# The prompt part of a hybrid GLA/MLA decoder step: stacked gate products, rope halves swapped by transfers, one fewer copy of the samples' queries

## The chip, the cores and the metric

One NeuronCore of a Trainium2 chip runs the kernel; the other cores are idle. The metric is device time in microseconds (us) of one execution, the median of several runs. TensorE does the matrix products, VectorE (DVE in the rows) and ScalarE (ACT) read its results out of the accumulator memory PSUM, GpSimd (POOL) and SyncE (SP) mostly issue transfers (DMA).

## What is computed

One decoder layer with two parallel head groups on one normed input `n` (512 prompt tokens, 16 meta tokens, 8 sample tokens of running sequences; width 1024), in single precision. Cut to what matters here:

```python
q, k, v, gr, g, cq, ckv, kpe = jnp.split(n @ w_in, idx, axis=-1)
lg = log_sigmoid((gr @ w_gk + b_gk)) / 16                  # gate logits, rank 16 -> 4 x 64
qh = (_rmsnorm(cq, q_norm) @ w_uq).reshape(B, T, 4, 128 + 64)
q_lat = einsum('bthn,rhn->bhtr', qh[..., :128], w_uk)
q_pe = _rope(qh[..., 128:])     # x1, x2 = halves: [x1*cos - x2*sin, x1*sin + x2*cos]
ckv, kpe = _rmsnorm(ckv, kv_norm), _rope(kpe)
# then chunked linear attention with the cumulative sums of lg, causal latent attention
# over the prompt, latent attention of the 8 samples over 4096 cached rows each (paged),
# merge by w_out, SwiGLU feed-forward, final norm
```

## The kernel before, in words

Everything stays in one fixed program per engine, ordered by hand; engines meet through semaphores. Big products are made exact enough by splitting both operands into a high and a low part of type fp32r and adding three products (high*high, low*high, high*low): `dense` (L753 to 763), `two_layers` (L766 to 778), `by_token` (L794 to 796) and `dense_piece` (L901 to 922). Each of those moves 256 to 268 columns and is one record in the trace. A plain fp32 product is two records. A weight block of 256 columns is loaded by SyncE (`load_block`), ScalarE copies its high part (`hi`, L1403) and VectorE subtracts for the low part (`lo`, L1776); two block buffers alternate, and `use(n)` on TensorE waits for `lo(n)`.

PSUM is used as four pairs of banks. `plan` writes down every result ("fill") in order and gives each the next pair in turn; `take(name)` on TensorE waits until the pair's earlier fill was read out (`free` on the reader), and `evacuated(name)` waits until a fill was read.

TensorE's order in the prompt part, which the change touches:

- transposes of the normed input (`xT`, L814), then `cq0` to `cq2` (the query latent);
- `tok0` to `tok2` (latent rows), then `ssq`: the sum over features of the squares of `cq`, made by multiplying three tiles of squares with a matrix of ones (`ones_sum`, L804, 6 products), then `tok3`, `tok4`;
- `kr` (rope part of the keys and the 16 gate features in one fill; ScalarE takes the key rows at L1451, VectorE the gate features into `grT` at L1830, which frees the pair), `wuk0`, `wuk1` and `kp` (transposes, L842 and L848);
- the gate logits `lg0` to `lg4`: one plain fp32 product per 128 tokens, 17 rows deep (16 features and a row of ones against the bias), 256 columns (L852). ScalarE and VectorE read each and go on to log-sigmoid;
- `qn0`, `qn1`, `qp0`, `qn2`, `qn3`, `qp1`: the queries of the heads, 18 split products each. ScalarE copies `qp` into `qpe` (L1466);
- small transposes (`cks`, `ck2`, L868 and L872), the samples' latent queries `qlat` (L880), then `sw0`, `sw1`: `qpe` multiplied by a permutation matrix so that the rope halves swap (L886, four plain fp32 products of 260 columns, 8 records); VectorE multiplies by sine and cosine and adds (L1860 to 1863) and signals `qpe_done`;
- the gates' cumulative sums `b0` to `b4` (L895);
- `q0` (48 split products as eight pieces), then `qx` (L940 and L945): the samples' queries spread over 128 rows, written twice, into two banks, 12 narrow fp32 products each, so that VectorE (L1882) and ScalarE (L1494) can each read its own bank and fill `Qall`; then `q1` (48 split products), then `snew` (L953);
- the loop over the cached rows, 16 steps (L968, L977, L991), with the products for `k`, `v` in between, fed by GpSimd's gathers of cache rows into a ring of six buffers (`gather_latent` L649, `gather_rope` L654).

What stands in the other queues around this: SyncE loads block 7, stores the latent rows (12 transfers, L528 and L529), and then waits for `q1` to load block 8. GpSimd fetches `w_gk` and `b_gk` (L659, L660), gathers the first rope rows once `ctok_done` is there, waits for `qpe_done`, clears two buffers (L665, L666) and then gathers on. VectorE runs in the order: gate logits, `lo(6)`, copies of `cks`, `ck2`, `qlat`, the rotation, `lo(7)`, transposes of cached keys (`cache_keys`, L1875), `Qall`.

## Time and profile before

| What | us |
|---|---|
| median of 3 runs | 862.75 |
| the three runs | 859.09, 863.98, 862.75 |
| the profiled execution, its own time | 864.38 |
| its span, first to last instruction | 862.6 |
| mean granted TensorE clock, as a share of full speed | 0.958 |

The profiled execution is one more run with the hardware profiler on; its span lies inside its own time. The page gives busy times by engine, the span in 40 slices, the chain of work that ended last and the costliest groups of instructions. Where the granted clock of a stretch is 1.00 TensorE runs at 2.4 GHz, where it is 0.50 at 1.2 GHz. A busy time of TensorE counts overlapping records once.

### The profile page before, as it was taken

To read this page: it belongs to the slowest core of one execution; us is meant where nothing else is said; L and a number is where in the kernel's file an instruction comes from. 1 tells how busy PE (TensorE), PEld (TensorE's weight loads), DVE (VectorE), ACT (ScalarE), POOL (GpSimd) and SP (SyncE) were. 2 spreads that over 40 slices of the span, in tenths; PEclk is the share of its full clock that TensorE was granted. 3 is DMA by queue.
4 is the path that set the end of the run, shared out by engine and by line. 5 is a ranking of instruction groups with operands and counts; after the bars stand their busy time and mean duration, and the time that the engine had idled before them with its cause. 6 is when DMAs were issued, how large, how long until landed. Compare 5 with 4: busy or idle time off the path is not lost.

```text
span 862.6 us, 20177 instructions
## 1 busy us (share of the span) xinstructions
PE 803.0 (93%) x8886; PEld 756.0 (88%) x8886; DVE 442.6 (51%) x596; ACT 268.8 (31%) x428; POOL 124.6 (14%) x147
## 2 busy tenths in 40 slices
PE   1999988788888899999999999999999999999997
PEld 1998987667776699788999999999999999999996
DVE  4344638676686556868346444445544454123223
ACT  5234312111123344545545322222222222223113
POOL 5101314343451022630000000000000000000000
PEclk9998979999999999689999999999999999999998
DMA  8525165876883022033431333322223332222202
GB/s 259 176 55 156 60 234 213 307 267 225 320 337 104 8 67 60 2 99 121 133 99 50 99 97 97 97 96 73 78 94 97 97 97 87 86 98 86 85 0 99
DMA packets 72160, 105.95 MB, mean 123 GB/s; under 512 B 7584, under 2 KB 63960, under 8 KB 67872
## 3 DMA queue, kind: packets, MB, share of 16 engines
q1 hardware_dynamic: 64528, 62.89, 23.2%
q0 software_dynamic: 7568, 42.11, 13.1%
q8 instruction: 52, 0.85, 0.4%
q14 instruction: 12, 0.10, 0.0%
HBM read 100.99 MB, written 4.00 MB: 122 GB/s over the span
## 4 chain that ended last, share of the span: by engine, by line
PE 85%; DVE 7%; issue 4%; ACT 2%; DMA 1%; SPq 0%; ACTq 0%; DVEq 0%
PE pair L776 10%; PE pair L777 10%; PE pair L778 10%; PE pair L761 8%; PE pair L762 8%; PE pair L763 8%; PE pair L968 4%; PE pair L991 2%; DVE KT L1875 2%; PE pair L1190 2%; PE pair L794 2%; PE pair L795 1%; PE pair L796 1%; PE pair L814 1%; DMA X<-in_x_prompt 1%
## 5 line engine op out<-in xcount | busy, mean ns | idle before, releaser
L776 PE MATMUL pair<-xhi,whi 128*128 128x260 f32 x736 | 209.2, 284 | 0.4 <-ACT rsf L1704 0.4
L777 PE MATMUL pair<-xlo,whi 128*128 128x260 f32 x736 | 208.6, 283 | 0.0
L778 PE MATMUL pair<-xhi,wlo 128*128 128x260 f32 x736 | 208.6, 283 | 0.0
L776 PEld LDWEIGHTS pair<-xhi,whi 128*128 128x128 f32 x736 | 139.6, 190 | 0.7 <-issue 0.6
L777 PEld LDWEIGHTS pair<-xlo,whi 128*128 128x128 f32 x736 | 139.6, 190 | 0.0
L778 PEld LDWEIGHTS pair<-xhi,wlo 128*128 128x128 f32 x736 | 139.5, 189 | 0.0
L763 PE MATMUL pair<-hhi,wlo 128*128 128x260 f32 x352 | 99.4, 282 | 0.0
L761 PE MATMUL pair<-hhi,whi 128*128 128x260 f32 x352 | 99.3, 282 | 0.0
L762 PE MATMUL pair<-hlo,whi 128*128 128x260 f32 x352 | 99.2, 282 | 0.0
L1875 DVE STREAM_TRANSPOSE KT<-KC 128x2048 uint32<-128x2048 uint32 x32 | 73.7, 2303 | 0.0
L2219 DVE TENSOR_TENSOR wlo<-wraw,whi 128x2048 fp32r<-128x2048 f32 x22 | 50.4, 2293 | 38.7 <-ACT whi L1724 38.7
L761 PEld LDWEIGHTS pair<-hhi,whi 128*128 128x128 f32 x352 | 66.3, 188 | 0.0
L762 PEld LDWEIGHTS pair<-hlo,whi 128*128 128x128 f32 x352 | 66.2, 188 | 0.0
L763 PEld LDWEIGHTS pair<-hhi,wlo 128*128 128x128 f32 x352 | 66.1, 188 | 0.0
L2244 DVE TENSOR_TENSOR wlo<-wraw,whi 128x2048 fp32r<-128x2048 f32 (+1 forms) x10 | 20.8, 2079 | 75.9 <-ACT whi L1736 75.9
L968 PEld LDWEIGHTS pair<-KT,Qall 128*32 128x32 f32 x2048 | 32.3, 110 | 21.9 <-DVE KTp L1876 10.0
L968 PE MATMUL pair<-KT,Qall 128*32 128x64 f32 x2048 | 37.8, 221 | 14.1 <-issue 7.8
L1719 ACT ACTIVATE hhi<-fe 128x520 f32 x22 | 13.7, 639 | 106.7 <-DVE fe L2232 106.7
L649 POOL DMA_INDIRECT KC<-in_cache_ckv,icur x32 | 31.3, 979 | 77.2 <-issue 72.1
L1724 ACT ACTIVATE whi<-wraw 128x2048 fp32r<-128x2048 f32 x22 | 41.8, 1902 | 0.0
L1776 DVE TENSOR_TENSOR wlo<-wraw,whi 128x2048 fp32r<-128x2048 f32 (+2 forms) x12 | 23.5, 1956 | 33.4 <-ACT whi L1403 33.3
L654 POOL DMA_INDIRECT KP<-in_cache_kpe,icur x32 | 31.4, 982 | 54.1 <-DVE ctok L1840 44.6
(351 smaller groups left out, 1671.0 us busy)
## 6 DMA issues: line engine op xcount, KB each, us to landing
wraw<-in_w_gate SPq DMA_DIRECT2D x11, 1024.0 KB, 5.3
wraw<-in_w_up SPq DMA_DIRECT2D x11, 1024.0 KB, 5.3
wraw<-in_w_down SPq DMA_DIRECT2D x8, 1024.0 KB, 5.2
X<-in_x_prompt SPq DMA_DIRECT2D x8, 512.0 KB, 5.6
wraw<-in_w_in SPq DMA_DIRECT2D x4, 1024.0 KB, 6.0
wsame<-in_w_in SPq DMA_DIRECT2D x4, 1024.0 KB, 6.2
wraw<-in_w_down SPq DMA_DIRECT2D x4, 768.0 KB, 4.8
wsame<-in_w_out SPq DMA_DIRECT2D x2, 1024.0 KB, 6.6
```

The source lines that it names most:

```text
L649: g.indirect_dma_start(KC[x][:, :], None, ckv_rows, bass.IndirectOffsetOnAxis(icur[x][:, 0:1], 0)).then_inc(S(f"kc_loaded{x}"), 16)
L654: g.indirect_dma_start(KP[x][:, :], None, kpe_rows, bass.IndirectOffsetOnAxis(icur[x][:, 0:1], 0)).then_inc(S(f"kc_loaded{x}"), 16)
L761: mm(out, wcols(h, j), hi[:, kx, tok], start=first and j == 0, stop=False)
L762: mm(out, wcols(h, j), lo[:, kx, tok], start=False, stop=False)
L763: ins = mm(out, wcols(l, j), hi[:, kx, tok], start=False, stop=last and j == len(k_of) - 1)
L776: mm(out, h[:, k, c], xhi[:, k, tok], start=k == order[0], stop=False)
L777: mm(out, h[:, k, c], xlo[:, k, tok], start=False, stop=False)
L778: ins = mm(out, l[:, k, c], xhi[:, k, tok], start=False, stop=k == order[-1])
L968: ins = mm(pairs[2][32 * t:32 * t + 32, o:o + 64], Qall[:, n // 2, 32 * c:32 * c + 32], kk, start=c == 0, stop=c == NBLK - 1)
L1724: f(whi[n % 2][:, :], wraw[n % 2][:, :], ACT.Copy).then_inc(w_hi, 1)
L1875: v_.transpose(KT[y][:, :, :, :].rearrange("p u c j -> p (u c j)").bitcast(U32), KC[x][:, :].bitcast(U32))
L2219: tt(wlo[n % 2][:, :], wraw[n % 2][:, :], whi[n % 2][:, :].bitcast(F32), ALU.subtract).then_inc(w_lo, 1)
```

## The change

The edits, in TensorE's order:

1. VectorE adds the three tiles of query squares (two additions, one before and one after `lo(3)`), and `ssq` is made from the sum: 2 products in place of 6.
2. The gate features are laid in `grs` as 96 rows: high part and a row of ones, low part, high part again with ones; `w_gk` and `b_gk` are loaded three times into `wgk`, and `wgr` holds their high part in rows 0 to 63 and their low part in rows 64 to 95. One fp32r product, 96 rows deep, then gives the sum of the three split products for 128 tokens. GpSimd clears more and issues six transfers in place of two; ScalarE gains two copies for the weights and two for the features, and VectorE a subtraction for the weights and one in place of the copy into `grT`. The pair of `kr` is freed by that last subtraction.
3. The five gate products run after `qn0` and not before it, in two fills `lg0` (four tiles of tokens) and `lg1`; their readers work on 1024 columns at a time in place of four times 256.
4. `sw0`, `sw1` and the permutation matrix go. SyncE swaps the rope halves of `qpe` into `rsw` by transfers within the on-chip memory, four for each `qp`, 32 rows of 520 numbers (65 KB) each, behind the 12 stores in its queue. VectorE waits for them in `rotate`: `rotate(0)`, `lo(7)`, `rotate(1)`.
5. The `qx` fill is written once, 12 narrow products in place of 24. VectorE and ScalarE read the same bank, ScalarE after VectorE.
6. With five fills fewer between `kr` and `b4`, the pairs of the fills shift: `b4` now has the pair that `q0` takes.

The diff, cut to its core:

```diff
--- before
+++ after
@@ -136,10 +135,8 @@
     put(*[f"xT{k}" for k in range(KD)], *[f"cq{m}" for m in range(3)])
-    put("tok0", "tok1", "tok2", "ssq", "tok3", "tok4", "kr", "wuk0", "wuk1", "kp", *[f"lg{i}" for i in range(NT)])
-    for hh in range(2):
-        put(f"qn{2 * hh}", f"qn{2 * hh + 1}", f"qp{hh}")
-    put("cks", "ck2", "qlat", "sw0", "sw1", *[f"b{c}" for c in range(NT)])
+    put("tok0", "tok1", "tok2", "ssq", "tok3", "tok4", "kr", "wuk0", "wuk1", "kp", "qn0", "lg0", "lg1", "qn1", "qp0", "qn2", "qn3", "qp1")
+    put("cks", "ck2", "qlat", *[f"b{c}" for c in range(NT)])
     turn[0] = 0
...
@@ -311,7 +308,7 @@
         vtok = sb("vtok", [P, NT, 512], at=v_at)
-        grT = sb("grT", [32, T], at=v_at + 10240)
+        grs = sb("grs", [96, T], F32R, at=v_at + 10240)
         q_at = v_at + 10240 + 4 * T
...
@@ -345,6 +342,7 @@
         sqs = sb("sqs", [P, 3, NQ], at=v_at)
+        rsw = sqs
         scrk = sb("scrk", [P, KVL], at=v_at + 12 * NQ)
...
@@ -383,7 +381,8 @@
-        wgk = sb("wgk", [32, 256], at=K_at + 36 * NQ)
+        wgk, wgr = (sb(name, [96, 256], dt, at=K_at + 36 * NQ) for name, dt in (("wgk", F32), ("wgr", F32R)))
+        wgh = sb("wgh", [96, 256], F32R, at=a)
         lgs = sb("lgs", [P, NT, 256], at=a)
...
@@ -527,6 +526,11 @@
                 sp.dma_start(dst_s[0, :, 0, :], ctok[0:NB, NT - 1, col:col + width]).then_inc(out_done, 16)
+            for hh in range(2):
+                sp.wait_ge(pair_free[pair_of(f"qp{hh}")], reads(f"qp{hh}") + 1)
+                for o in range(0, P, ROPE):
+                    for d0, s0 in ((o, o + HALF), (o + HALF, o)):
+                        sp.dma_start(rsw[d0:d0 + HALF, hh, :], qpe[s0:s0 + HALF, hh, :]).then_inc(S(f"sw_loaded{hh}"), 16)
             for n in range(B_V, B_UKV + 1):
...
@@ -625,7 +629,11 @@
             g.memset(xlo_f[:, KD * XW:KD * XW + XPAD].bitcast(F32), 0.0).then_inc(S("pad_done"), 1)
-            g.memset(grT[:, :], 1.0).then_inc(S("pad_done"), 1)
+            pool.wait_ge(S("pad_done"), 2)
+            g.memset(grs[:, :].bitcast(F32), 1.0).then_inc(S("gr_set"), 1)
+            pool.wait_ge(S("gr_set"), 1)
+            g.memset(grs[32:64, :].bitcast(F32), 0.0).then_inc(S("gr_set"), 1)
+            pool.wait_ge(S("gr_set"), 2)
             g.memset(krT[:, T:TPAD], 0.0).then_inc(S("kr_pad"), 1)
...
@@ -656,8 +664,10 @@
             pool.wait_ge(pe_done, fills(f"xT{KD - 1}"))
-            pool.dma_start(wgk[0:RANK, :], w_gk[0]).then_inc(S("wgk_loaded"), 16)
-            pool.dma_start(wgk[RANK:RANK + 1, :], b_gk).then_inc(S("wgk_loaded"), 16)
+            link(g.memset(wgk[:, :], 0.0))
+            for r in (0, 32, 64):
+                pool.dma_start(wgk[r:r + RANK, :], w_gk[0]).then_inc(S("wgk_loaded"), 16)
+                pool.dma_start(wgk[r + RANK:r + RANK + 1, :], b_gk).then_inc(S("wgk_loaded"), 16)
             pool.wait_ge(S("ctok_done"), NT + 1)
...
@@ -814,7 +824,7 @@
                 done(ins)
-            pe.wait_ge(S("pad_done"), 3)
+            pe.wait_ge(S("pad_done"), 2)
...
@@ -827,8 +837,8 @@
             pe.wait_ge(c2_loaded, 16)
-            pe.wait_ge(S("sqs_done"), 3)
-            done(ones_sum(take("ssq"), [sqs[:, k, :] for k in range(3)]))
+            pe.wait_ge(S("sq_sum"), 2)
+            done(ones_sum(take("ssq"), [sqs[:, 0, :]]))
             for i in range(3, NT):
...
@@ -847,20 +857,25 @@
             done(ins)
-            def gates(i):
...
-                done(mm(take(f"lg{i}")[0:TT[i], 0:256], grT[0:RANK + 1, P * i:P * i + TT[i]], wgk[0:RANK + 1, :], start=True, stop=True))
...
-            evacuated("kr")
-            pe.wait_ge(S("wgk_loaded"), 32)
-            for i in range(NT):
-                gates(i)
+            def gates():
...
+                pe.wait_ge(S("wg_done"), 1)
+                evacuated("kr")
+                pe.wait_ge(S("gr_copy"), 1)
+                ps = take("lg0")
+                for i in range(NC):
+                    ins = mm(ps[:, 256 * i:256 * i + 256], grs[:, P * i:P * i + P], wgr[:, :], start=True, stop=True)
+                done(ins)
+                done(mm(take("lg1")[0:TT[4], 0:256], grs[:, 4 * P:T], wgr[:, :], start=True, stop=True))
...
             pe.wait_ge(S("qnlo_done"), 1)
...
                     layer(f"qn{2 * hh + x}", n, P * x, 3, qnhi, qnlo)
+                    if hh == 0 and x == 0:
+                        gates()
                 done(dense(take(f"qp{hh}"), view(whi, n), view(wlo, n), cols(2 * P), list(range(3)), qnhi, qnlo))
...
@@ -879,17 +894,10 @@
             done(ins)
-            for hh in range(2):
-                ps = take(f"sw{hh}")
-                evacuated(f"qp{hh}")
-                for half in range(2):
-                    ins = mm(ps[:, 512 * half:512 * half + QH], C("swap"), qpe[:, hh, QH * half:QH * half + QH], start=True, stop=True)
-                done(ins)
...
             def gate_sums(c):
                 ps = take(f"b{c}")
-                pe.wait_ge(S("lgs_done"), c + 1)
+                pe.wait_ge(S("lgs_done"), 1 if c < NC else 2)
                 tri = C("ucum") if c < 4 else C("ucum4", TT[4])
...
@@ -934,15 +942,14 @@
             wide = lambda at: rep[:, at // 32, :, :].rearrange("p g j -> p (g j)")
-            for bank in (0, 512):
-                for c in range(8):
-                    o = bank + 32 * c
-                    ins = mm(ps[:, o:o + 32], wide(32 * (c % 4)), qlT[:, c // 4, :, :].rearrange("p h b -> p (h b)"), start=True, stop=True)
-                for e in range(2):
-                    for aa in range(2):
-                        o = bank + 256 + 32 * e
-                        out = ps[:, o:o + 32].rearrange("p (q a b) -> p q a b", q=2, a=2)[:, :, aa, :]
-                        ins = mm(out, wide(64 * aa + 32 * e), qpe[:, :, SA:NQ], start=True, stop=True)
+            for c in range(8):
+                o = 32 * c
+                ins = mm(ps[:, o:o + 32], wide(32 * (c % 4)), qlT[:, c // 4, :, :].rearrange("p h b -> p (h b)"), start=True, stop=True)
+            for e in range(2):
+                for aa in range(2):
+                    o = 256 + 32 * e
+                    out = ps[:, o:o + 32].rearrange("p (q a b) -> p q a b", q=2, a=2)[:, :, aa, :]
+                    ins = mm(out, wide(64 * aa + 32 * e), qpe[:, :, SA:NQ], start=True, stop=True)
             done(ins)
...
@@ -953,7 +960,7 @@
             evacuated("qx")
-            evacuated("sw0")
+            evacuated("b3")
             pe.wait_ge(S("ps_clear"), 2)
...
@@ -1445,22 +1452,30 @@
             hi(4)
+            act.wait_ge(S("wgk_loaded"), 16 * 6)
+            f(wgh[64:96, :], wgk[64:96, :], ACT.Copy)
+            f(wgr[0:64, :], wgk[0:64, :], ACT.Copy).then_inc(S("wg_high"), 1)
             link(f(stat[:, 24:24 + NT], stat[:, 16:16 + NT], ACT.Ln, scale=1.0 / KVL, bias=C("eps")))
...
             ins.then_inc(S("kr_done"), 1)
+            act.wait_ge(S("gr_set"), 2)
+            f(split2(grs[ROPE:ROPE + RANK, :]), halves(ready("kr"), T)[ROPE:ROPE + RANK], ACT.Copy).then_inc(S("gr_hi"), 1)
+            act.wait_ge(S("gr_hi"), 1)
+            f(grs[0:RANK, :], grs[ROPE:ROPE + RANK, :].bitcast(F32), ACT.Copy).then_inc(S("gr_copy"), 1)
             hi(5)
...
                 free(f(wukT[:, 2 * x:2 * x + 2, :].rearrange("p a b -> p (a b)"), ready(f"wuk{x}")[:, 0:512], ACT.Copy), f"wuk{x}")
-            act.wait_ge(S("lgt_clear"), 1)
-            for i in range(NT):
-                f(lgt[0:TT[i], i, :], ready(f"lg{i}")[0:TT[i], 0:256], ACT.Abs).then_inc(S("lga_done"), 1)
             for hh in range(2):
...
                     free(f(split2(qnT[:, 2 * hh + x, :]), halves(ready(f"qn{2 * hh + x}")), ACT.Copy), f"qn{2 * hh + x}")
+                    if hh == 0 and x == 0:
+                        f(lgt[:, 0:NC, :].rearrange("p i c -> p (i c)"), ready("lg0")[:, 0:1024], ACT.Abs).then_inc(S("lga_done"), 1)
+                        act.wait_ge(S("lgt_clear"), 1)
+                        f(lgt[0:TT[4], NC, :], ready("lg1")[0:TT[4], 0:256], ACT.Abs).then_inc(S("lga_done"), 1)
                 if hh == 0:
-                    act.wait_ge(S("lga_done"), NT)
+                    act.wait_ge(S("lga_done"), 2)
                     link(f(lgt[:, :, :], lgt[:, :, :], ACT.Exp, scale=-1.0))
...
@@ -1489,7 +1504,7 @@
-                ps = pairs[pair_of("qx")][:, 512:832].rearrange("p (c h b) -> p b c h", c=NBLK, h=MH)
+                ps = pairs[pair_of("qx")][:, 0:320].rearrange("p (c h b) -> p b c h", c=NBLK, h=MH)
                 out = Qall[:, :, :].rearrange("p b (c d x) -> p b c d x", d=2, x=16)[:, :, :, 1, 4 * gg:4 * gg + 4]
...
@@ -1497,6 +1512,7 @@
             ready("qx")
+            act.wait_ge(S("Qall_done"), NG)
             for gg in range(NG - 1):
...
@@ -1800,7 +1816,12 @@
                 free(v_.tensor_copy(split2(cq[:, m, :]), halves(ready(f"cq{m}"))), f"cq{m}")
+            dve.wait_ge(S("sqs_done"), 2)
+            tt(sqs[:, 0, :], sqs[:, 0, :], sqs[:, 1, :], ALU.add).then_inc(S("sq_sum"), 1)
             lo(3)
+            dve.wait_ge(S("sqs_done"), 3)
+            dve.wait_ge(S("sq_sum"), 1)
+            tt(sqs[:, 0, :], sqs[:, 0, :], sqs[:, 2, :], ALU.add).then_inc(S("sq_sum"), 1)
             dve.wait_ge(small_loaded, 16)
...
@@ -1820,14 +1841,15 @@
             lo(4)
+            dve.wait_ge(S("wg_high"), 1)
+            tt(wgr[64:96, :], wgk[64:96, :], wgh[64:96, :].bitcast(F32), ALU.subtract).then_inc(S("wg_done"), 1)
             dve.wait_ge(S("rk_done"), 1)
...
             ps = ready("kr")
-            dve.wait_ge(S("kr_done"), 1)
-            dve.wait_ge(S("pad_done"), 3)
-            free(v_.tensor_copy(split2(grT[0:RANK, :]), halves(ps, T)[ROPE:ROPE + RANK]), "kr")
+            dve.wait_ge(S("gr_hi"), 1)
+            free(tt(split2(grs[32:32 + RANK, :]), halves(ps, T)[ROPE:ROPE + RANK], split2(grs[ROPE:ROPE + RANK, :]).bitcast(F32), ALU.subtract), "kr")
             dve.wait_ge(c2_loaded, 16)
...
@@ -1840,31 +1862,29 @@
             lo(5)
-            for i in range(NT):
-                n = TT[i]
-                dve.wait_ge(S("lga_done"), i + 1)
-                free(ts(lgs[0:n, i, :], ready(f"lg{i}")[0:n, 0:256], 0.0, None, ALU.min), f"lg{i}")
+            dve.wait_ge(S("lga_done"), 2)
+            free(ts(lgs[:, 0:NC, :].rearrange("p i c -> p (i c)"), ready("lg0")[:, 0:1024], 0.0, None, ALU.min), "lg0")
+            free(ts(lgs[0:TT[4], NC, :], ready("lg1")[0:TT[4], 0:256], 0.0, None, ALU.min), "lg1")
             lo(6)
             dve.wait_ge(S("lgt_done"), 1)
-            for i in range(NT):
-                n = TT[i]
-                dve.wait_ge(pair_free[pair_of(f"lg{i}")], reads(f"lg{i}") + 1)
-                tt(lgs[0:n, i, :], lgs[0:n, i, :], lgt[0:n, i, :], ALU.subtract).then_inc(S("lgs_done"), 1)
+            for x, n, tiles in ((0, P, slice(0, NC)), (1, TT[4], slice(NC, NT))):
+                dve.wait_ge(pair_free[pair_of(f"lg{x}")], reads(f"lg{x}") + 1)
+                tt(lgs[0:n, tiles, :], lgs[0:n, tiles, :], lgt[0:n, tiles, :], ALU.subtract).then_inc(S("lgs_done"), 1)
             free(v_.tensor_copy(cks[:, :, :], ready("cks")[:, 0:64].rearrange("p (j t) -> p j t", j=2)[:, :, 0:NB]), "cks")
...
             free(v_.tensor_copy(qlT[:, :, :, :], ps[:, 0:64].rearrange("p (r h b) -> p r h b", r=2, h=4)), "qlat")
-            for hh in range(2):
-                ps = ready(f"sw{hh}")
-                dve.wait_ge(S("qn_done"), 1)
-                free(tt(split2(rsb[:, :]), halves(ps), split2(C("sinf")), ALU.mult), f"sw{hh}")
+            def rotate(hh):
...
+                dve.wait_ge(S(f"sw_loaded{hh}"), 16 * 4)
+                dve.wait_ge(pair_free[pair_of(f"qp{hh}")], reads(f"qp{hh}") + 1)
+                link(tt(rsw[:, hh, :], rsw[:, hh, :], C("sinf"), ALU.mult))
                 link(tt(qpe[:, hh, :], qpe[:, hh, :], C("cosf"), ALU.mult))
-                dve.wait_ge(pair_free[pair_of(f"sw{hh}")], reads(f"sw{hh}") + 1)
-                ins = tt(qpe[:, hh, :], qpe[:, hh, :], rsb[:, :], ALU.add)
-                if hh == 0:
-                    link(ins)
-            ins.then_inc(S("qpe_done"), 1)
+                return tt(qpe[:, hh, :], qpe[:, hh, :], rsw[:, hh, :], ALU.add)
...
+            rotate(0)
             lo(7)
+            rotate(1).then_inc(S("qpe_done"), 1)
```

## Rows read from the trace of the kernel before

**Rows 1.** the page: busy times, and TensorE's granted clock in 40 slices.

```profile
PE 803.0 (93%) x8886; PEld 756.0 (88%) x8886; DVE 442.6 (51%) x596; ACT 268.8 (31%) x428; POOL 124.6 (14%) x147
...
PEclk9998979999999999689999999999999999999998
```

**Rows 2.** TensorE's waits, whole span: us, times, longest.

```profile
PE pair L814 <- ACT X L1417: 17.3, 1, 17.3
PE pair L968 <- issue: 11.7, 8, 2.9
```

**Rows 3.** the chain, 55 to 125 us: start us, us, what.

```profile
55.54 2.63 PE pair L804 x12
...
69.66 0.12 PE pair L763
...
71.43 2.83 PE pair L852 x8
...
75.89 0.52 PE pair L761
...
90.82 0.23 PE pair L868 x2
...
93.77 3.45 PE pair L886 x8
...
99.83 0.32 PE pair L915
...
105.80 1.70 PE pair L940 x16
...
108.38 1.80 PE pair L940 x16
...
111.43 0.41 PE pair L915
...
119.98 0.67 PE pair L953 x24
```

**Rows 4.** four stretches: PE, PEld, DVE, ACT, POOL busy; clock; DMA share; GB/s.

```profile
76.00:79.00 3.00, 3.00 (x14) 3.00 (x15) 0.41 (x1) 0.31 (x1) 0.65 (x1) 0.50 1.02 317
80.00:90.00 10.00, 10.00 (x86) 10.00 (x85) 2.36 (x2) 7.04 (x8) 0.00 (x0) 1.00 0.31 101
94.00:97.00 3.00, 3.00 (x8) 2.33 (x8) 1.29 (x3) 0.00 (x0) 0.00 (x0) 0.52 0.00 0
...
111.00:117.00 6.00, 6.00 (x29) 6.00 (x29) 2.50 (x9) 1.89 (x4) 1.60 (x3) 0.50 1.01 411
```

**Rows 5.** VectorE in order of time, 40 to 125 us.

```profile
70.57 0.71 DVE L1830 COPY grT<-pair 16x536 f32<-16x536 f32 x1 [1.63 <-PE pair L842]
...
93.81 0.23 DVE L1856 COPY qlT<-pair 128x64 f32<-128x64 f32 x1 [1.25 <-PE pair L880]
...
99.16 0.70 DVE L1863 TENSOR_TENSOR qpe<-qpe,rsb 128x520 f32<-128x520 f32 x1
99.78 2.28 DVE L1776 TENSOR_TENSOR wlo<-wraw,whi 128x2048 fp32r<-128x2048 f32 x1
...
111.55 1.92 DVE L1882 TENSOR_SCALAR Qall<-pair,cst 128x320 f32<-128x320 f32 x4 [6.67 <-PE pair L945]
```

**Rows 6.** ScalarE in order of time, 40 to 125 us.

```profile
90.86 0.61 ACT L1466 ACTIVATE qpe<-pair 128x520 f32<-128x520 f32 x1 [1.55 <-PE pair L763]
```

**Rows 7.** GpSimd in order of time, 0 to 180 us.

```profile
27.78 0.54 POOL L659 DMA_DIRECT2D wgk<-in_w_gk  x1 [2.10 <-PE pair L814]
...
99.92 0.53 POOL L665 MEMSET PS<- 128x512 f32 x1 [23.27 <-DVE qpe L1863]
```

**Rows 8.** SyncE's queue in order of time.

```profile
74.90 3.01 SPq L528 DMA_DIRECT2D out<-ctok  x5
```

**Rows 9.** transfers issued 45 to 60 us: KB each, us to landing.

```profile
wraw<-in_w_uq SPq DMA_DIRECT2D x4, 96.0 KB, 2.8
```

**Rows 10.** VectorE's waits from 120 to 280 us.

```profile
DVE fin L1906 <- PE pair L968: 44.2, 16, 5.6
```

More of the change, by code:

```diff
@@ L72 @@
 _at = 0
-for _name, _n in (("ident", P), ("eps", 1), ("gap", 7), ("ones", P), ("ucum", P), ("swap", P), ("cosf", NQ), ("sinf", NQ), ("cosk", NT * ROPE),
+for _name, _n in (("ident", P), ("eps", 1), ("gap", 7), ("ones", P), ("ucum", P), ("room", P), ("cosf", NQ), ("sinf", NQ), ("cosk", NT * ROPE),
                   ("sink", NT * ROPE), ("ucum4", 24), ("sell", 4), ("selo", 4), ("quart", 1), ("cap", P + T - SA), ("same", 16)):
@@ L336, in hybrid_decode_kernel @@
         KTp = [sb(f"KTp{i}", [P, UNITS, 2, 32], at=K_at + 16384 + 2048 * i) for i in range(2)]
-        assert 4 * (CC["ucum4"][0] - CC["swap"][0]) >= 7168 and rope_at % 32 == 0
+        assert 4 * (CC["ucum4"][0] - CC["room"][0]) >= 7168 and rope_at % 32 == 0
         PS = [sb(f"PS{i}", [P, 16, 32], at=rope_at + 2048 * i) for i in range(2)]
```

7 lines of the change are left out of this document (3 added, 4 removed).

## The prediction

> **What bounds the kernel now.** I read the page first: TensorE is busy for 803.0 of 862.6 us, more than any other engine, and its clock line has a few low slices in the first half [rows 1]. Then TensorE's waits: past the first load (17.3 us) the long ones lie in the loop over the cached rows (L968) [rows 2]. So in the prompt part TensorE hardly waits, and what leaves its stream there leaves the span, provided that nothing else takes over. Third, the chain in order of time: from 55 to 120 us it is TensorE's own work almost piece by piece, the gate products, the swap products and both banks of `qx` among it [rows 3]. Fourth, the granted clock of stretches: 0.50 from 76 to 79, 0.52 from 94 to 97 and 0.50 from 111 to 117 us, against 1.00 from 80 to 90 [rows 4]. Each low stretch follows work that is no dense stream: the transposes, waits and 17-row gate products after `kr`; the small transposes and `qlat` (90.82 to 93.77); the 48 narrow records of `qx` (105.80 to 111.43) [rows 3]. At the upper clock a split product takes 10/86 = 0.116 us, at the lower one 3/14 = 0.214 us [rows 4].
>
> **The change part by part**, against the profiled execution.
>
> 1. Query squares. `ssq` was 12 records in 2.63 us, 0.219 each [rows 3]; 8 of them go: **-1.75 us**. VectorE's two additions are of the size of the rotation's (0.70 each [rows 5]), 1.4 us together, both done before TensorE has made `tok0` to `tok2` (72 split products, 8.3 us from 0.116 each); with that cover gone they would cost at most 1.4.
>
> 2. Gates. The ten records and the wait between them ran from 71.43 to 75.89, 4.46 us on the chain [rows 3]. Five split products come instead: 0.60. No row has a split product 96 rows deep; I bound it by the 128-row one, 0.116 at the upper and 0.214 at the lower clock, and by the old gate record, 2.83/8 = 0.354 [rows 3, 4], so 0.6 to 1.8 for five, and take the 128-row one at the upper clock, the nearest in type and width. In return `qn0` needs the pair of `kr`, which is released later: before by VectorE's copy alone (0.71 [rows 5]), now by a ScalarE copy of 16 rows (as that of `qp`, 0.61 [rows 6]) and then a subtraction like the old copy. That is +0.60 (0 if ScalarE is free at once and the copies overlap, 1.3 if the hand-over costs another 0.7). Net **-3.26 us**. The further ScalarE copy into rows 0 to 15 delays `hi(5)` and the copies of `wuk` by 1.2 us; `lg0` and `lg1` need those pairs, but stand behind `qn0`'s 18 x 0.116 = 2.1 us. The weights' two copies and one subtraction lie in the time in which both engines wait for `kr`. GpSimd's six transfers at 0.54 each take 3.2 us from 27.78 [rows 7]; it has nothing else to do until `ctok_done`. Its added clears are of the size of the one at 99.92 (0.53 [rows 7]), two of them, while it waits for the constants anyway.
>
> 3. `qn0` ran wholly at the lower clock after the gates. Now it follows `kr` with about 2 us of transposes and waits between, so I take it at the upper: 18 x (0.214 - 0.116) = **-1.76 us** (0 if the clock falls all the same).
>
> 4. Swap products. They took 3.45 us, nearly all at the lower clock [rows 3, 4]; 8 records at 0.219 are 1.75. What leads to that low stretch (the small transposes and `qlat`) is unchanged, so I expect the stretch to stay and to lie on `b0` to `b4` and the start of `q0` instead: the removal brings the 1.75, not the 3.45. `q0` must now wait until `b4` is read (ScalarE, some 0.3 us). **-1.45 us**, with 0 and -3.45 as ends.
>
> 5. `qx` once: from 108.38 to 111.43 goes, **-3.05 us** [rows 3]. ScalarE's copies follow VectorE's 1.92 us [rows 5] and take no longer, so `Qall` is complete some 4 us after `qx`; TensorE asks for it after `q1`, 6 us later. Without that cover it costs 1.9.
>
> 6. `q1` took 8.55 us (111.43 to 119.98), most of it at the lower clock; `q0`, of the same size, took 5.97 (99.83 to 105.80) [rows 3, 4]. With only 24 narrow records (2.6 us) before it, I take `q1` at `q0`'s time: **-2.58 us** (0 to -2.58).
>
> The larger `lg0`, `lg1` reads are fewer instructions over the same columns and lie beside `qn1` to `qn3`.
>
> What the transfers must meet: by items 1 to 3 the copy of `qp1`, 90.86 plus 0.61, comes 6.8 earlier, at 84.7 [rows 6]. SyncE stands free by then: its 12 stores go out at 3.01/5 = 0.60 each from 74.90 [rows 8] (now earlier), the loads behind it wait for `q1`. Four issues at 0.60 end at 87.1. No row shows a transfer from on-chip memory to on-chip memory; the nearest, 96 KB weight loads, land 2.8 us after issue [rows 9], so 89.9. VectorE copies `qlat` at 93.81 - 6.8 = 87.0, then `rotate(0)` (3 x 0.70), `lo(7)` (2.28) and `rotate(1)`: `qpe_done` at 93.7, against 99.86 before [rows 5]. `qx` starts at 105.80 - 8.2 = 97.6. So the transfers cost nothing while the last lands by 95.5, and have 5.6 us to spare.
>
> The Trainium skill ("DMA: Bandwidth & Descriptors", the table under "Anatomy of one DMA") speaks against this part: each transfer has about 2.0 us of fixed time, and it advises to join small ones. By an estimate from that page four in a row, none overlapping, would land after 4 x 2.15 = 8.6 us, and 3.4 us of the spare time would go, with the sum unchanged; that is what lifts the chance of the slower rival below from almost nothing.
>
> Sum: 1.75 + 3.26 + 1.76 + 1.45 + 3.05 + 2.58 = 13.85 us. All of it comes before the loop, whose stages release each other (VectorE waits 44.2 us in it for TensorE's scores [rows 10]), so I let it through whole. The profiled execution would come to 864.4 - 13.8 = 850.6; its own time stands 1.6 above the median of the runs, so the median forecast is 862.75 - 13.8 = **849.0 us**.
>
> **The rivals.**
>
> A. *The clock falls again.* The low stretches behind items 3 and 6 come back, since there is still non-dense work of 2 to 2.6 us before `qn0` and `q1`, and 2.95 us sufficed at 90.82. For: the likeness in length. Against: both are shorter than any that was followed by a low stretch. It costs 1.76 + 2.58 = 4.3: 853.3 us. Chance 0.22.
>
> B. *The loop goes at the gathers' pace.* GpSimd's next gathers wait for `qpe_done` (its clears stood at 99.92 [rows 7]), which comes only 6.2 us earlier, while TensorE comes 13.8 earlier. If the ring's filling decides, only 6.2 arrives at the end: 856.5. For: the gathers move much data. Against: VectorE, which takes the ring's buffers, waits for TensorE and for no gather [rows 10]. Chance 0.10.
>
> C. *Slower: the swap transfers come late.* `rotate(0)` stands on VectorE before `lo(7)`, the first cached keys and `Qall`, and everything after it waits. This decides from a landing after 95.5, and the result turns slower than before from 95.5 + 13.8 = 109.3, that is if the eight transfers take 22 us longer than reckoned (say 24: 865). Only a queue that is held up elsewhere could do that. Chance 0.03.
>
> D. *The change doesn't free TensorE*: the late release of `kr`, or `b4`'s pair, waits as long as the gates and swaps took (4.5 + 1.75 more than reckoned, so some 7.5 saved): 855. Chance 0.05.
>
> **How the numbers follow.** The forecast has 0.60, and the four rivals 0.40. Low end: the 94 to 97 stretch vanishes too (another 1.75, 847.2) and the runs scatter, the lowest before lying 3.7 below the median; I take 2.7 of that, 844.5. High end: rival B, 857. It holds A, B and D. About half a per cent, 4.3 us, is what a measurement can tell from no change, so all but C and an outlying B are faster: 0.94, same 0.03, slower 0.03.
>
> **What would show it.** In the chain after: no gate products before `qn0`, no swap products, 24 records for `qx`. The clock 1.00 over `qn0` and `q1`, one low stretch over `b` and the start of `q0`. TensorE idle about 1 us before `qn0`, for VectorE's subtraction. The last swap transfer landed by about 90 us, `qx` without a wait. `snew` near 106 us in place of 119.98. The loop as long as before. Wrong would be a wait of TensorE for `qpe_done`, a VectorE that waits for gathers, or a loop longer by several us.

## The result and the profile after

| What | before | after |
|---|---|---|
| median, us | 861.66 (4 runs, 859.09 to 863.98) | 847.88 (4 runs, 846.82 to 850.86) |
| ratio, with its 95% interval | 1 | 0.984 (0.9808 to 0.9872) |
| the profiled execution, own time and span | 864.38, 862.6 | 848.68, 846.9 |
| mean granted clock | 0.958 | 0.969 |

The kernel is 13.8 us faster, 1.6%; the interval allows 11.0 to 16.5. The forecast was 849.0. One more run of the kernel before makes its median 861.66.

The page after, its busy times and clock slices, against [rows 1]:

```profile
PE 785.7 (93%) x8841; PEld 740.7 (87%) x8841; DVE 445.1 (53%) x593; ACT 270.4 (32%) x429; POOL 125.4 (15%) x153
...
PEclk9999999999999997699999999999999999999998
```

TensorE has 17.3 us less to do. The low slices from 64 to 86 and 108 to 129 us (8 and 7 in [rows 1]) are gone; the two behind the loop are there in both kernels (7 and 6 from 318 to 360 us here, 6 and 8 from 345 to 388 before).

TensorE's waits over the whole span (us, times, longest), against [rows 2]:

```profile
PE pair L824 <- DVE X L1807: 18.7, 1, 18.7
PE pair L975 <- issue: 8.2, 6, 2.5
```

The only wait that has grown in the prompt part is the one before `qn0`, 1.0 us where the gates waited 0.3 (read below). The first load is 1.4 us later than in the profile of before; the change doesn't touch it, and it scatters (the same kernel has 17.1 in e9).

The chain, 54 to 112 us, against [rows 3]:

```profile
56.98 0.88 PE pair L814 x4
...
69.35 0.14 PE pair L773
...
69.80 0.38 ACT krT L1461
70.20 0.62 ACT grs L1464
70.92 0.72 DVE grs L1852
...
71.77 0.36 PE pair L771
74.17 0.47 PE pair L867 x4
...
86.54 1.88 PE pair L895 x16
88.42 2.45 PE pair L903 x20
90.89 0.22 ACT bT L1486
91.16 0.40 PE pair L923
...
97.19 1.70 PE pair L947 x16
98.90 0.88 PE pair L952 x8
99.78 0.21 PE pair L923
...
105.63 0.68 PE pair L960 x24
```

From `ssq` to `snew` it is 105.63 - 56.98 = 48.65 us, where it was 64.44 [rows 3]. Read it from above: `ssq` is 4 records; between `kr` (ends 69.49) and `qn0` (71.77) TensorE makes the transposes and then waits 1.0 us for ScalarE's copy of `kr` and VectorE's subtraction behind it; then `qn0`, the five gate products, no swap products between `qlat` (L895) and `b` (L903), a short hand-over to `q0` by ScalarE's read of `bT`, 24 records of `qx`, and `q1` in 5.85 us.

The same stage in stretches (busy time of PE, PEld, DVE, ACT, POOL; clock; DMA share; GB/s), against [rows 4]:

```profile
71.00:74.00 3.00, 2.23 (x18) 2.26 (x19) 2.94 (x7) 2.75 (x4) 0.18 (x1) 1.00 0.06 18
...
86.00:89.00 3.00, 3.00 (x27) 2.80 (x26) 1.44 (x5) 1.99 (x2) 0.00 (x0) 1.00 0.27 66
...
100.00:106.00 6.00, 6.00 (x65) 5.85 (x65) 2.39 (x9) 2.23 (x5) 4.53 (x8) 1.00 1.01 411
```

All are at 1.00, over `qn0`, `b` and `q1` alike.

SyncE in order of time, the same transfers with their size and the median us from issue to landing, then VectorE and GpSimd in order of time:

```profile
81.61 7.02 SPq L533 DMA_DIRECT2D sqs<-qpe  x8
```

```profile
sqs<-qpe SPq DMA_DIRECT2D x8, 65.0 KB, 2.2
```

```profile
88.60 0.69 DVE L1881 TENSOR_TENSOR sqs<-sqs,cst 128x520 f32<-128x520 f32 x1
...
92.88 0.69 DVE L1881 TENSOR_TENSOR sqs<-sqs,cst 128x520 f32<-128x520 f32 x1
```

```profile
95.10 0.53 POOL L675 MEMSET PS<- 128x512 f32 x1 [18.11 <-DVE qpe L1883]
```

The swap transfers are issued from 81.61 to 88.63; the last one, whose issue takes 0.59 us and so begins at 88.04, lands 2.0 us later (the median of the eight is 2.2), at 90.0. VectorE begins `rotate(0)` at 88.60 and `rotate(1)` at 92.88 with no wait before either, and GpSimd's clears, which wait for `qpe_done`, start at 95.10 (99.92 before [rows 7]).

### The profile page after: what moved, and what is told of

Its sections match the earlier page's. It is cut to its first block, busy times and chain, and to the rows that moved or that the text cites. A ratio compares the mean times of both kernels' runs of the same rounds, so it can differ in the third digit from the quotient of the medians.

```text
span 846.9 us, 20095 instructions
## 1 busy us (share of the span) xinstructions
PE 785.7 (93%) x8841; PEld 740.7 (87%) x8841; DVE 445.1 (53%) x593; ACT 270.4 (32%) x429; POOL 125.4 (15%) x153
## 4 chain that ended last, share of the span: by engine, by line
PE 85%; DVE 7%; issue 4%; ACT 2%; DMA 1%; SPq 0%; ACTq 0%; DVEq 0%
PE pair L786 11%; PE pair L787 10%; PE pair L788 10%; PE pair L771 8%; PE pair L773 8%; PE pair L772 8%; PE pair L975 4%; PE pair L998 2%; PE pair L804 2%; PE pair L1197 2%; DVE KT L1895 2%; PE pair L806 1%; PE pair L805 1%; PE pair L824 1%; DMA X<-in_x_prompt 1%
## 5 line engine op out<-in xcount | busy, mean ns | idle before, releaser
L1752 ACT ACTIVATE whi<-wraw 128x2048 fp32r<-128x2048 f32 (+1 forms) x10 | 17.5, 1745 | 68.3 <-PE pair L773 68.3
```

## The experiments

They ran four at a time on three chips (e1 to e4, e5 to e8, e9 to e12), each time with the kernel before beside them. There both kernels take 39 to 50 us more than above, nearly all of it in the loop (see the last section), so only kernels of one chip are compared, and stages are read rather than whole spans. The table has them all. "ssq to snew" is the prompt part that the change touches, by the records' starts; "first scores" is from `snew` to VectorE's first maximum over the scores (L1926); "loop" is from `snew` to the transposes behind the last scores. These three columns are from one profiled execution each, which can lie off the median of its kernel: that of e9 took 888.38 (median 897.89), that of e11 896.62 (median 889.64). Behind the loop, where no edit reaches, the profiles differ as well: 583 to 584 us in e1 to e9, 588 to 589 in e10 to e12.

| Run | median | ratio to before | ssq to snew | first scores | loop |
|---|---|---|---|---|---|
| before (as above) | 861.66 | 1 | 64.53 | 8.3 | 156.0 |
| after (as above) | 847.88 | 0.984 | 48.74 | 5.3 | 154.7 |
| e1_after_again | 886.49 | 0.979 (0.975 to 0.983) | 50.33 | 6.0 | 197.4 |
| e2_qx_twice | 893.79 | 0.987 (0.983 to 0.991) | 54.53 | 7.4 | 199.4 |
| e3_swap_products | 890.39 | 0.983 (0.978 to 0.988) | 51.61 | 5.3 | 198.3 |
| e4_old_gates | 893.80 | 0.987 (0.982 to 0.991) | 55.58 | 7.9 | 201.1 |
| e5_after_beside | 889.46 | 0.980 (0.976 to 0.984) | 48.74 | 8.8 | 201.7 |
| e6_before_beside | 907.33 | 0.999 (0.996 to 1.002) | 63.00 | 8.0 | 201.9 |
| e7_gathers_late | 893.54 | 0.985 (0.981 to 0.989) | 48.74 | 12.3 | 205.0 |
| e8_transfers_x4 | 899.55 | 0.992 (0.989 to 0.994) | 61.66 | 5.4 | 197.9 |
| e9_after_third | 897.89 | 0.986 (0.984 to 0.988) | 50.26 | 7.8 | 198.9 |
| e10_gathers_early | 896.32 | 0.985 (0.983 to 0.988) | 48.75 | 5.3 | 197.3 |
| e11_early_joined | 889.64 | 0.976 (0.973 to 0.978) | 50.83 | 5.3 | 201.2 |
| e12_gates_first | 902.47 | 0.989 (0.985 to 0.993) | 52.91 | 9.2 | 205.3 |

### The changed kernel again, and with one part undone

**e1_after_again**, no edit.

> The changed kernel unaltered, as the yardstick of this call. It comes to about 848 us (846 to 851). Theory 1 (the low-clock stretches of the prompt part came from the removed work) expects the granted clock at 1.00 from `kr` to the first step of the loop again. Theory 2 (in the one profile seen, the stretch over the gate sums was missed by luck of timing, since the work ahead of it, small transposes and `qlat`, is unchanged) expects a stretch at 0.50 over `b0` to `b4` or the start of `q0` in some profiles of this and the kernels beside it, at a cost of about 1.75 us each time.

Measured 0.979; the 848 us expected didn't come, since this chip runs both kernels slower. There is a stretch at the lower clock where the prediction had left one. 86 to 89 us, columns as above:

```profile
86.00:89.00 3.00, 3.00 (x16) 2.77 (x15) 2.93 (x4) 1.49 (x4) 0.00 (x0) 0.53 0.09 22
```

`b0` to `q0` took 4.48 us where the profile above has 2.88, and the stage 50.33 for 48.74. So the stretch that the prediction expected exists, in some executions and not in others of the same kernel.

**e2_qx_twice**: the second bank of `qx` again, with ScalarE reading it.

```diff
-            for c in range(8):
-                o = 32 * c
+            for bank in (0, 512):
+                for c in range(8):
+                    o = bank + 32 * c
...
-            act.wait_ge(S("Qall_done"), NG)
```

> Undoes the single `qx` alone: 24 narrow products in two banks again, VectorE and ScalarE each on its own. Theory 1 (length of the narrow run brings the clock down): `qx` 5.6 us in place of 2.6 and `q1` 8.5 in place of 5.85, so 5.7 us longer than the changed kernel, about 853.5. Theory 2 (a low stretch there needs something else, such as the earlier stretches): only the 3.05 us of the second bank come back, `q1` stays at 5.85, about 851.

Measured: 7.3 us longer than e1. In its profile `qx` takes 5.95 and `q1` 8.37 us. The seven microseconds over the second bank and most of `q1`:

```profile
98.00:105.00 7.00, 7.00 (x35) 7.00 (x34) 2.51 (x9) 1.89 (x4) 4.39 (x7) 0.51 1.02 411
```

35 matmul records in 7 us: the end of the second bank and most of `q1` at half speed, as in [rows 4]. The stage is 5.8 us longer than the undisturbed 48.74, against 3.05 + 2.58 = 5.6 for items 5 and 6. Both terms stand: the products removed and the clock over what follows them.

**e3_swap_products**: the permutation products `sw0`, `sw1` back on TensorE and the transfers gone; all else changed.

```diff
+            for hh in range(2):
+                ps = take(f"sw{hh}")
+                evacuated(f"qp{hh}")
+                for half in range(2):
+                    ins = mm(ps[:, 512 * half:512 * half + QH], C("swap"), qpe[:, hh, QH * half:QH * half + QH], start=True, stop=True)
+                done(ins)
```

> Undoes the transfers alone: the four permutation products come back before the gate sums, with VectorE's rotation from the accumulator. Theory 1 (the products themselves cost little but lie where the clock falls): the stretch at 0.50 returns behind `qlat`, the products take 3.45 us, 851.4 in all. Theory 2 (the stretch is not tied to them): the clock stays at 1.00, they take 8 x 0.219 = 1.75 us, 849.7.

Measured: 3.9 us longer than e1 by the medians; the stage is 2.9 us longer than the undisturbed one. The products ran from 86.39 to 88.23, 1.84 us, and the clock over them:

```profile
86.00:89.00 3.00, 3.00 (x20) 2.77 (x20) 1.64 (x4) 0.24 (x2) 0.00 (x0) 1.00 0.00 0
```

At the upper clock they cost 1.84, the 1.75 that the prediction had worked out. Of the other 1 us, half is a new hand-over: the last of `b` needs the banks of `sw1`, which VectorE's rotation reads late, and `b` takes 3.34 for 2.88 us. The other half lies in `q1` (6.52 for 5.93), where TensorE stops once on "issue", for 0.32 us at 105.6; this has no visible link to the edit. The 3.45 of [rows 3] were these products in a low stretch, and here they run without one: the stretch doesn't belong to the products.

**e4_old_gates**: the 17-row gate products before `qn0`, as before; the other parts changed.

```diff
+            evacuated("kr")
+            pe.wait_ge(S("wgk_loaded"), 32)
+            for i in range(NT):
+                done(mm(take(f"lg{i}")[0:TT[i], 0:256], grT[0:RANK + 1, P * i:P * i + TT[i]], wgk[0:RANK + 1, :], start=True, stop=True))
```

> Undoes the gates alone: five plain fp32 products, 17 rows deep, before `qn0`. Theory 1 (they cost their own time and bring the clock down for `qn0`): 3.24 + 1.73 = 5.0 us longer than the changed kernel, 852.9, with `qn0` at 0.50 and 4.1 us. Theory 2 (the fall is not theirs): 3.2 us longer, 851.1, `qn0` in 2.3 us. If their low stretch also decides whether the later ones occur, the clock over the gate sums falls too.

Measured: 7.3 us longer than e1. Gates and wait take 4.4 us, and the lower clock lies over `qn0` behind them; a second low stretch lies over `b` (4.10 for 2.88). The chain, 65 to 80 us:

```profile
72.80 1.04 PE pair L858 x2
73.85 0.52 PE pair L767
74.36 0.21 PE pair L768
```

The split products of `qn0` follow each other at 0.21 to 0.22 us. The stage is 6.8 us longer than the undisturbed one: 5.0 are items 2 and 3 (3.24 and 1.73 as measured below), 1.2 the second stretch, 0.4 a longer wait for VectorE's copy `grT` (0.73 for the 0.32 of before), and 0.25 more in the queries (15.17 us for the 14.92 of before).

### The waits that the change could have made

**e5_after_beside** and **e6_before_beside**, the two kernels as they are, on the second chip.

> The changed kernel again, as the yardstick for the two beside it, since the chip of the last call ran all kernels some 40 us slower in the loop over the cached rows. Theory 1 (the whole saving lies before the loop): `ssq` to `snew` takes 48.7 us with the upper clock throughout, 50.3 with one low stretch over the gate sums, on any chip, and 14 to 16 us less than the kernel before beside it. Theory 2 (part of the saving on the slower chip came out of the loop): its loop is several us shorter than that of the kernel before.

> The kernel before, unaltered, for a second profile of it beside the changed one. Theory 1: `ssq` to `snew` takes 64.5 us again, with low-clock stretches after the gate products and after `qx`; the stretch over the swap products may be missing, which would make it 1.7 us shorter. Loop equal to that of the changed kernel within 2 us. Theory 2: the loop is longer than the changed kernel's by 3 us or more.

Measured: 0.980 and 0.999. The loop is 201.65 us in the one and 201.88 in the other, so in this pair nothing is won or given back in it: `ssq` to `snew` differs by 14.3 us. The medians differ by 17.9, and the other 3.6 us these two profiles don't place (the profiled execution of e6, 901.27, was the fastest of its ten).

**e7_gathers_late**: GpSimd clears a buffer eleven times more before its gathers.

```diff
+            for _ in range(11):
+                link(g.memset(PS[0][:, :, :], 0.0))
             g.memset(PS[0][:, :, :], 0.0).then_inc(S("ps_clear"), 1)
```

> The changed kernel, with eleven more clears by GpSimd, one after another, between `qpe_done` and the next gathers, so that these start some 6 us later. Theory 1 (the loop releases its own gathers, and the ring's first fill is early enough): the time stays within 1 us of the changed kernel. Rival B of the prediction (the loop goes at the gathers' pace from their start): 6 us longer.

Measured: 4.1 us longer than e5. The stage is the same to 0.01 us, and only the gathers start later, by some 6 us. TensorE in order of time, at the first scores:

```profile
103.73 0.75 PE L962 MATMUL pair<-cst,prod 128*8 128x1 f32 x24
...
106.33 0.71 PE L977 MATMUL pair<-KT,Qall 128*32 128x64 f32 x23
107.48 0.31 PE L977 MATMUL pair<-KT,Qall 128*32 128x64 f32 x3 [0.44 <-issue]
108.23 0.31 PE L977 MATMUL pair<-KT,Qall 128*32 128x64 f32 x5 [0.44 <-issue]
109.65 0.39 PE L977 MATMUL pair<-KT,Qall 128*32 128x64 f32 x5 [1.10 <-issue]
111.07 0.44 PE L977 MATMUL pair<-KT,Qall 128*32 128x64 f32 x5 [1.04 <-issue]
112.50 0.80 PE L977 MATMUL pair<-KT,Qall 128*32 128x64 f32 x20 [0.98 <-issue]
```

The idle time is no wait for data: the profile gives "issue" as its end, between products of one group whose operands were all there. In this stretch the 16 DMA engines are full (columns as above):

```profile
104.00:113.00 9.00, 4.78 (x92) 3.83 (x92) 3.06 (x3) 0.44 (x1) 6.14 (x9) 0.82 1.02 390
```

The first scores come 3.5 us later than in e5 (12.3 for 8.8), and most of that remains to the end. Rival B's price was the pace at which the ring fills; what is seen is another thing: the burst of gathers meets the load of block 8, and at the same time TensorE stalls at the start of the loop, for 4.0 us in all in the lines above. That the one causes the other is not shown. Full DMA engines don't bring such stalls each time: in the profile after they are as full at the first scores (1.01 from 106 to 111 us), and TensorE runs through. An obvious candidate is untested: the page of every run lists DMA queues of instructions too (`q8 instruction: 52, 0.85, 0.4%`, that is packets and MB), so TensorE may be waiting here for its own instructions.

**e8_transfers_x4**: each swap transfer cut into four of 130 columns, 32 in all.

```diff
+                        for c0 in range(0, NQ, NQ // 4):
+                            sp.dma_start(rsw[d0:d0 + HALF, hh, c0:c0 + NQ // 4], qpe[s0:s0 + HALF, hh, c0:c0 + NQ // 4]).then_inc(S(f"sw_loaded{hh}"), 16)
```

> The changed kernel, with each swap transfer cut into four of 130 numbers a row: 32 in place of 8, the same bytes. Theory 1 (their price is SyncE's issue, 0.6 us each, then 2.8 us to landing, and only what exceeds the spare time counts): the last lands at about 103.6 us in place of 91, `qpe_done` comes at 105.7, `qx` waits and starts 8.7 us later: 8.7 us longer in all. Theory 2 (what counts is the bytes, and the queue takes the smaller ones faster): less than 2 us longer.

Measured: 10.1 us longer than e5. SyncE's queue, and VectorE's two waits:

```profile
78.94 20.88 SPq L534 DMA_DIRECT2D sqs<-qpe  x32
```

```profile
90.91 0.70 DVE L1882 TENSOR_TENSOR sqs<-sqs,cst 128x520 f32<-128x520 f32 x1 [4.94 <-DMA sqs<-qpe]
...
101.04 0.70 DVE L1882 TENSOR_TENSOR sqs<-sqs,cst 128x520 f32<-128x520 f32 x1 [5.75 <-DMA sqs<-qpe]
```

32 transfers take 20.88 us to issue, 0.65 each, and the last, whose issue began at 99.23, is there when VectorE starts, 101.04 - 99.23 = 1.8 us later. `qx` starts 9.2 us later than in e5, and it is worse than that: TensorE waits 9.0 us, the granted clock falls during the wait, and `qx` takes 5.11 for 2.59 and `q1` 7.17 for 5.94, 3.7 us more. The first scores then come 3.4 us earlier behind `snew` than in e5 (5.4 for 8.8). This is rival C made real. In the changed kernel the last transfer has landed by 90.0. VectorE would wait for it from 92.88 on, 2.9 us later, and TensorE from another 2.1 on (`qpe_done` at 95.04, `qx` at 97.19).

### Towards a better version

**e9_after_third**, no edit, on the third chip.

> The changed kernel as it is, as yardstick for the three beside it. Both theories expect a ratio to the kernel before of 0.979 to 0.984 (0.984, 0.979 and 0.980 so far) and 48.7 us from the start of ssq to the start of snew, or 50.3 us if the stretch at the lower clock lies over b0 to b4 and q0, as it did in one of three profiles. The first reduce of the step loop ends its wait between 5.3 us (quiet) and 8.8 us (TensorE stalled between the score products) after snew.

Measured 0.986, just above the 0.979 to 0.984 expected, so the ratio of one pair of kernels varies from chip to chip by more than its interval on one chip says. This profile has another low stretch, over the first part of `q1`, which took 7.46 us:

```profile
98.00:101.00 3.00, 3.00 (x16) 3.00 (x15) 1.71 (x8) 1.72 (x4) 2.42 (x4) 0.50 1.01 423
```

**e10_gathers_early**: three gathers pulled ahead of the wait for the rope queries.

```diff
-            pool.wait_ge(S("qpe_done"), 1)
-            g.memset(PS[0][:, :, :], 0.0).then_inc(S("ps_clear"), 1)
-            g.memset(PS[1][:, :, :], 0.0).then_inc(S("ps_clear"), 1)
             pool.wait_ge(out_done, 16 * 12)
+            pool.wait_ge(pe_done, fills("ck2"))
             gather_latent(2)
-            gather_rope(2)
             pool.wait_ge(w_lo, B_V)
+            gather_latent(3)
+            gather_rope(3)
+            gather_latent(4)
+            gather_rope(4)
+            pool.wait_ge(S("qpe_done"), 1)
+            gather_rope(2)
+            g.memset(PS[0][:, :, :], 0.0).then_inc(S("ps_clear"), 1)
+            g.memset(PS[1][:, :, :], 0.0).then_inc(S("ps_clear"), 1)
```

> The gathers of steps 3 and 4 are issued ahead of the wait for the rope queries, and the one of step 2 behind ck2's products, so the five requests that in the changed kernel are issued between 96.5 and 106 us are out by about 98. Theory 1 (what the gathers cost is that their burst meets the load of block 8 and the first score products, when TensorE stalls for its instructions): the stalls at the first scores go, snew to first reduce is 5.3 us, and the time is 0 to 3.5 us shorter than the yardstick's, by as much as the yardstick's own first reduce lies over 5.3 us after snew. Theory 2 (the gathers never cost anything in the changed kernel; the delayed run was slow since it was delayed too far): the same time within 0.5 us. Either way ssq to snew stays at 48.7 us (or 50.3 with the low stretch).

Measured: 896.32 for 897.89, and ratios of 0.9852 and 0.9859: no difference that can be told. VectorE's first two maxima, in e9 and then in e10:

```profile
112.16 0.29 DVE L1926 TENSOR_REDUCE fin<-pair 128x1 f32<-128x128 f32 x1 [3.10 <-PE pair L975]
...
123.70 0.29 DVE L1926 TENSOR_REDUCE fin<-pair 128x1 f32<-128x128 f32 x1 [5.11 <-remote]
```

```profile
108.73 0.29 DVE L1931 TENSOR_REDUCE fin<-pair 128x1 f32<-128x128 f32 x1 [1.45 <-PE pair L980]
...
121.91 0.29 DVE L1931 TENSOR_REDUCE fin<-pair 128x1 f32<-128x128 f32 x1 [6.75 <-remote]
```

The first step does what the first theory said: 5.3 us after `snew` for 7.8. But the second maximum comes 18.5 us after `snew` for 19.3: 1.7 of the 2.5 us are given back one step later. That the gain goes further along in the loop is what the waits suggest: TensorE waits on "issue" before scores 19 times for 6.6 us in all, in e9 7 times for 2.7. Over the whole loop the profile of e10 is 1.6 us shorter (197.3 for 198.9), and behind the loop 5.6 us longer (588.9 for 583.3), which no edit explains; both executions were the fastest of their runs. The change of 0.2% in the medians is less than this measurement can tell, so the time decides for neither theory; what is shown is that the stalls at the entry can be moved, not whether it pays.

**e11_early_joined**: as e10, and `wuk0`, `wuk1` in one pair of banks.

```diff
-            for x in range(2):
-                ps = take(f"wuk{x}")
-                for y in range(2):
+            ps = take("wuk")
+            for y in range(4):
```

> As the run with early gathers, and wuk0 and wuk1 are made one fill, so that TensorE writes them in one pair of banks and qn0 need not wait until ScalarE and VectorE have copied kr. Theory 1 (the wait of 1.0 us before qn0 is the late release of kr's pair that the prediction costed at 0.60): kr's end to qn0 is 1.3 us instead of 2.3, ssq to snew 47.4 to 47.8 us, the time 1.0 to 1.3 us shorter than the run with early gathers alone. Theory 2 (qn0 then waits for its normalised queries instead, which come by way of VectorE): the wait stays within 0.3 us of 1.0 with another releaser, and the time is the same.

TensorE behind `kr`:

```profile
68.37 0.52 PE L862 MATMUL pair<-cst,krT 64*128 64x64 f32 x5
68.83 0.39 PE L776 MATMUL pair<-qnhi,whi 128*128 128x260 f32 x1
```

No wait stands before `qn0`; in e9 and e10 it is 0.97 and 0.98 us, released by VectorE's subtraction. So that wait was the late release of `kr`'s pair. `lg1` then waits 0.17 for ScalarE, and from the start of `kp` to that of `cks` it is 14.52 us for e9's 15.21: 0.69 of the 1.0 us stays. The medians say more, 6.7 us less than e10, ratio 0.976 for 0.985, with intervals that don't touch. What makes the other 5 to 6 us isn't shown: the profiled execution of e11 was the slowest of its five (896.62), with low stretches over `b` and over `q1`. On this chip it is faster than both kernels and than e10, and has the lowest ratio of this study; that the joined transposes bring more than 0.7 us rests on the medians of one chip alone.

**e12_gates_first**: the stacked gate products ahead of `qn0`.

```diff
+            gates()
             pe.wait_ge(S("qnlo_done"), 1)
...
-                    if hh == 0 and x == 0:
-                        gates()
```

> The five stacked gate products are put back ahead of qn0; all else is the changed kernel. They still need kr's copy, so what they take now stands between kr and the queries. Theory 1 (their new place cost little or nothing, the saving is that there are 5 and not 36 of them): 0 to 0.6 us longer than the yardstick, qn0 2.4 us. Theory 2 (the place matters through the clock: the short gate products before qn0 bring the lower clock over it, as 36 of them did): qn0 takes 4.1 us, the time is 1.7 to 2.3 us longer than the yardstick.

Measured: 4.6 us longer than e9. TensorE in order of time:

```profile
69.03 0.71 PE L867 MATMUL pair<-wgr,grs 96*128 96x256 f32 x4 [0.98 <-DVE grs L1850]
70.61 0.41 PE L869 MATMUL pair<-wgr,grs 96*24 96x256 f32 x1 [0.87 <-ACT wukT L1468]
71.19 0.56 PE L771 MATMUL pair<-qnhi,whi 128*128 128x260 f32 x1 [0.17 <-ACT wukT L1468]
```

(The 36 in the expectation is a slip: the old gate products were the ten records of item 2.) Two effects. TensorE waits 0.87 and 0.17 us for ScalarE's copies of `wuk`, which stand behind `hi(5)`: 1.0 us that e9 doesn't have (the 0.98 for VectorE stands before `qn0` there). And the lower clock comes over the last gate product, `qn0`, whose 18 products take 4.03 us in place of 2.24, and the start of `qn1`: 3.1 us. From `kp` to `cks` it is 19.38 for 15.21. The cover that item 2 named (the gates stand behind `qn0`) is worth these 4.2 us, more than either theory gave it: theory 2 left out the wait for `wuk` and the part of the low stretch outside `qn0`.

## Why the prediction was right

The step "what leaves TensorE's stream leaves the span" holds: the terms, each from the chains before and after, in us.

| Term | forecast | measured | from |
|---|---|---|---|
| 1 squares | -1.75 | -1.75 | 2.63 to 0.88 |
| 2 gates, with `kr`'s release | -3.26 | -3.24 | 4.46 gone, 0.59 and 0.63 in its place |
| 3 `qn0`'s clock | -1.76 | -1.73 | 71.77 to 74.17 for 4.13 |
| 4 swap products | -1.45 | -3.32 | 3.45 gone, 0.13 back |
| 5 `qx` once | -3.05 | -3.04 | 5.63 to 2.59 |
| 6 `q1`'s clock | -2.58 | -2.70 | 8.55 to 5.85 |
| sum | -13.85 | -15.78 | 64.44 to 48.65 |

- The profiled executions differ by 15.7 us of span: 15.8 of this sum, a start 1.4 later and a rest 1.35 shorter. The medians differ by 13.8. The profile of before was 2.7 us slower than its median, that of after 0.8; the interval on the ratio holds both sums.
- So the match of 13.8 with 13.85 is in part luck. The terms as this pair of profiles shows them sum to 15.8, 1.9 more than forecast, all of it in item 4, and how much of it an execution gets depends on low stretches that come and go: the stage took 48.74, 50.33, 48.74 and 50.26 us in the four profiles of the changed kernel, 64.53 and 63.00 in the two of the kernel before, a difference of 14.2 by the means.
- **The mis-sized term is item 4.** It said: "What leads to that low stretch ... is unchanged, so I expect the stretch to stay". In the profile after, it is gone, and the whole 3.45 with it, the upper end that the prediction had kept (-3.45). But the step wasn't simply wrong: e1 has the stretch just there, and it costs 1.6 us. Of the four profiles of the changed kernel (after, e1, e5, e9) two have no low stretch from `ssq` to `snew`, one has it over `b`, one over `q1`, and e7 and e10, whose TensorE work up to `snew` is the same, have none (48.74 and 48.75 us); both profiles of the kernel before (the one above and e6) have three, from within the gate products on, over the swap products and over `q1`. One execution is no basis for a term that hangs on one such stretch.
- Rival A (the clock falls again, 4.3 us) came true in part, in one profile of four: e9's `q1`, 1.5 us. Over `qn0` it never fell except where the gates were put before it (e4, e12).
- Rival B (the gathers' pace) didn't decide. Late gathers do cost (e7), at the entry into the loop, where TensorE stops on "issue" and not for an empty ring.
- Rival C needed late transfers. The last landed at 90.0, in a profile that starts `ssq` 1.4 us later, so at 88.6 on the forecast's clock, where 89.9 was forecast: the row of 2.8 us to landing counts from the start of an issue, and the forecast added it to the end of the last one; and these took 2.0. They have 2.9 + 2.1 = 5.0 us to spare before TensorE waits, where 5.6 was forecast. (The rival's "22 us longer than reckoned" is 109.3 less the end of the issues, 87.1; from the landing at 89.9 it is 19.4.)
- The Trainium skill ("DMA: Bandwidth & Descriptors", the table under "Anatomy of one DMA") has about 2.0 us fixed for a transfer; the table is of GpSimd's path, and these went by SyncE's queue. As the time to land, 2.0 us from issue, the trace is near it; as a cost of each of several in a row it isn't, since 32 smaller ones took 0.65 each to issue (e8).
- Rival D: the late release of `kr` was +0.63, forecast +0.60; `b4`'s pair made `q0` wait 0.3, as forecast.

## What to carry to other kernels

Count what leaves the busy engine's stream and then the clock over what comes behind it. Of the 15.8 us here, items 1, 2, 5 and the 1.62 of item 4 make 9.7; but 0.5 of that is the low end of the second bank of `qx` (3.05 for 2.59), and 0.9 the low clock over the gate products (eight records took 2.83, in e4, where the clock fell later, 1.96). So about 8.3 us were instructions at the speed of the upper clock and 7.5 the lower clock gone. Putting five short products behind a dense group, and not before it, was worth 4.2 us (e12). A low stretch that one profile shows may be missing from the next profile of the same kernel, so profile twice before a term rests on it. Small transfers within the chip are cheap while something covers them, but their queue took 0.65 us to issue each, and a wait they cause costs a second time through the clock (e8).
